# Moving adaLN weight slabs between slots of the RWKV turns, two score-maxima calls into the last turn, and eight square sums behind four more matmul pieces

## What is computed (the reference, cut)

```python
# RWKV heads, after the scan y:
mean = jnp.mean(y, axis=-1, keepdims=True)
yc = y - mean
y = yc * lax.rsqrt(jnp.mean(yc * yc, axis=-1, keepdims=True) + RWKV_GN_EPS)
# dilated attention: scores, then their maximum, then the exponential
m = jnp.max(scores, axis=-1, keepdims=True)
p = jnp.exp(scores - m)
# differential attention of the second block, the norm of each head's output
y = of * lax.rsqrt(jnp.mean(jnp.square(of), axis=-1, keepdims=True) + RMS_EPS) * g * (1.0 - lam_init)
```

## Time and profile before

| | us |
|---|---|
| median of 3 runs | 3110.01 |
| lowest, highest | 3106.93, 3116.91 |
| time of the profiled execution | 3103.57 |
| its span, first to last instruction | 3101.8 |
| TensorE busy | 3001.1 (97%) |
| DVE busy | 1669.6 (54%) |
| ACT busy | 1352.2 (44%) |
| mean granted TensorE clock | 0.989 of full |

### The profile page before, as it was taken

How to read it: one execution, slowest core, us unless ns; L and a number is a source line. 1 busy time by engine, 2 the same in 40 slices (tenths; PEclk the granted TensorE clock), 3 DMA queues, 4 the chain that set the end, 5 groups by cost and what they waited for, 6 DMA issues and landing times.

```text
span 3101.8 us, 48573 instructions
## 1 busy us (share of the span) xinstructions
PE 3001.1 (97%) x19912; PEld 2541.9 (82%) x19912; DVE 1669.6 (54%) x2561; ACT 1352.2 (44%) x2084; POOL 43.8 (1%) x84
## 2 busy tenths in 40 slices
PE   8999998999899999999999999999999999999997
PEld 7877876898588778788888887788888998889896
DVE  6655655544666556564454224554562574256754
ACT  5333333434455445454443224444442461255543
POOL 1000000000000000000000000000000000000000
PEclk9999999999999999999999999999999999999998
DMA  7655655355665776745553222222233442234443
GB/s 273 218 205 208 216 185 214 105 172 224 236 217 188 273 272 233 283 165 180 184 188 113 88 89 82 82 82 92 82 128 107 165 171 87 95 121 148 137 163 109
DMA packets 73800, 510.18 MB, mean 164 GB/s; under 512 B 8325, under 2 KB 8465, under 8 KB 19601
## 3 DMA queue, kind: packets, MB, share of 16 engines
q1 hardware_dynamic: 63504, 435.74, 40.8%
q0 software_dynamic: 10112, 71.73, 6.0%
HBM read 503.23 MB, written 6.55 MB: 164 GB/s over the span
## 4 chain that ended last, share of the span: by engine, by line
PE 91%; DVE 4%; ACT 2%; DMA 2%; issue 1%; SPq 0%; ACTq 0%; DVEq 0%
PE bank L767 21%; PE bank L711 16%; PE bank L710 7%; PE bank L1467 5%; PE bank L1469 5%; PE bank L1468 5%; PE bank L910 3%; PE bank L942 3%; PE bank L911 2%; PE bank L912 2%; PE bank L1050 2%; DMA ring_f<-in_w_mod 2%; PE bank L808 2%; PE bank L809 1%; PE bank L810 1%; PE bank L1118 1%
## 5 line engine op out<-in xcount | busy, mean ns | idle before, releaser
L2285 DVE TENSOR_TENSOR ring_f32r<-ring_f,high_f32r 128x1024 fp32r<-128x1024 f32 (+1 forms) x738 | 830.2, 1163 | 761.9 <-ACT high_f32r L1642 745.4
L1642 ACT CAST high_f32r<-ring_f 128x1024 fp32r<-128x1024 f32 (+1 forms) x644 | 609.3, 994 | 859.0 <-PE bank L767 462.6
L711 PE MATMUL bank<-hyz_f32r,high_f32r 128*128 128x512 f32 x2112 | 752.6, 401 | 3.8 <-DVE hyz_f32r L2285 3.8
L710 PE MATMUL bank<-hyz_f32r,ring_f32r 128*128 128x256 f32 x2008 | 564.8, 281 | 1.8 <-DVE ring_f32r L2285 0.9
L767 PE MATMUL bank<-hyz_f32r,high_f32r 128*128 128x512 f32 (+1 forms) x2016 | 534.9, 343 | 5.2 <-DVE hyz_f32r L2285 3.0
L711 PEld LDWEIGHTS bank<-hyz_f32r,high_f32r 128*128 128x128 f32 x2112 | 394.4, 188 | 122.4 <-issue 34.9
L767 PE MATMUL bank<-hyz_f32r,ring_f32r 128*128 128x512 f32 (+1 forms) x1184 | 411.1, 347 | 0.0
L767 PEld LDWEIGHTS bank<-hyz_f32r,high_f32r 128*128 128x128 f32 x2016 | 348.6, 190 | 49.2 <-issue 6.2
L710 PEld LDWEIGHTS bank<-hyz_f32r,ring_f32r 128*128 128x128 f32 x2008 | 380.4, 189 | 7.6 <-DVE hyz_f32r L2285 1.6
L1467 PE MATMUL bank<-hyz_f32r,high_f32r 128*128 128x512 f32 (+1 forms) x1024 | 359.0, 351 | 2.7 <-DVE ring_f32r L2285 2.7
L1469 PE MATMUL bank<-hyz_f32r,ring_f32r 128*128 128x512 f32 (+1 forms) x1024 | 344.8, 337 | 0.0
(11 more groups left out here) (415 smaller groups left out, 4022.7 us busy)
## 6 DMA issues: line engine op xcount, KB each, us to landing
ring_f<-in_w_in SPq DMA_DIRECT2D x159, 1024.0 KB, 4.9
ring_f<-in_w_up SPq DMA_DIRECT2D x88, 1024.0 KB, 4.9
ring_f<-in_w_out SPq DMA_DIRECT2D x56, 1024.0 KB, 4.9
ring_f<-in_w_mod SPq DMA_DIRECT2D x48, 1024.0 KB, 5.1
ring_f<-in_w_down SPq DMA_DIRECT2D x64, 704.0 KB, 4.1
h_f<-in_w_mod POOLq DMA_DIRECT2D x38, 1024.0 KB, 6.8
ring_f<-in_w_kv SPq DMA_DIRECT2D x8, 1024.0 KB, 5.5
z_f<-in_w_mod POOLq DMA_DIRECT2D x8, 1024.0 KB, 8.2
```

Of the source, the lines that this page charges most:

```text
L710: mm(small, lo, x_hi, start=False, stop=False)
L711: last = mm(bank, hi, pair(x_hi, x_lo), start=start, stop=stop)
L1642: act.copy(w_hi[p % 2][:, half], slot[s % SLOTS][:, half]).then_inc(w_high, 1)
L2285: return v.tensor_tensor(out, in0, in1, op)
```

## The change

The 1st place of each turn is taken out and a new last place is put behind the next turn's first products (`ups_matmuls`), in turn 5 behind `a_scores(0)` and `a_v_turned(0)`; the numbering moves down by one, so that the same slabs are read in the same order. `MOD_STEPS` follows. Before `rw_ops` TensorE takes 7.9 instead of 7.0 us of steps (6.9 instead of 6.0 in the last turn, where `evacuated(2)` has 2.4 instead of 3.2). The two first calls of `a_maxima` move into DVE's last turn, between the group norm's variance and the wait for its root. In layer 1 the sum of squares comes 8 instead of 4 pieces behind the values; the pieces behind it are fewer by 4. Layer 0 stays as it was.

```diff
--- before.py
+++ after.py
@@ -49,7 +49,7 @@
 IN1_EARLY = 6
 IN1_FIRST, IN1_COUNT = (6, 13, 20, 27, 34, 40), (7, 7, 7, 7, 6, 6)
 IN1_LAST = 46
-MOD_STEPS = (31, 50, 57, 65, 73, 82, 91, 103)
+MOD_STEPS = (31, 57, 66, 75, 82, 91, 104, 109)
 TURN_MODS = 8
 NORM_MODS = (8, 4)
 UP_MODS = [3, 6, 9, 12] + [32 + 3 * k // 2 for k in range(16)] + [62 + 4 * k // 3 for k in range(16)]
@@ -1086,10 +1086,9 @@
                 if final:
                     beside1(4.0)
                     sgu_sum("g_made", sgu_t, 1)
-                    beside1(6.0)
+                    beside1(6.9)
                 else:
-                    beside1(7.0)
-                turn_mod(TURN_MODS * i + 1)
+                    beside1(7.9)
                 pe.wait_ge(S("rw_ops"), i + 1)
 
                 def rows(n):
@@ -1108,7 +1107,7 @@
                                       kn[rows(hd), t * P + 64 * j:t * P + 64 * j + 64], start=True, stop=True)
                 last.then_inc(S("rw_prod"), 1)
                 beside1(2.6)
-                turn_mod(TURN_MODS * i + 2)
+                turn_mod(TURN_MODS * i + 1)
                 pe.wait_ge(S("rw_bonus"), i + 1)
                 pe.wait_ge(S("inv_dve"), i * 10 + 1)
 
@@ -1122,12 +1121,12 @@
 
                 def evacuated(dve, act=None):
                     if final and dve in (2, 3):
-                        beside1(3.2 if dve == 2 else 0.0)
+                        beside1(2.4 if dve == 2 else 0.0)
                         sgu_turned(dve - 2)
                     elif final and dve in (5, 7):
                         sgu_mixed(dve // 2 - 2)
                     elif dve in (4, 8):
-                        turn_mod(TURN_MODS * i + 2 + dve // 4)
+                        turn_mod(TURN_MODS * i + 1 + dve // 4)
                     else:
                         beside1(1.6 if dve == 10 else 1.8 if final and dve == 6 else 1.15)
                     pe.wait_ge(S("inv_dve"), i * 10 + dve)
@@ -1180,7 +1179,7 @@
                             last = mm(bk[(5, 2)[j]][rows(hd), t * CH:(t + 1) * CH], tok_vz[rows(j), 1, t, rows(hd)],
                                       m_tt[rows(j), 2 * hd + t, :], start=True, stop=True)
                 last.then_inc(S("rw_nv"), 1)
-                turn_mod(TURN_MODS * i + 5)
+                turn_mod(TURN_MODS * i + 4)
                 pe.wait_ge(S("rw_v_made"), 2 * i + 1)
                 for t in range(2):
                     for hd in range(2):
@@ -1198,7 +1197,7 @@
                     mm(bk[6][:, c * CH:(c + 1) * CH], state, zr[:, t, 1, o:o + 64], start=True, stop=True
                        ).then_inc(S("ch_u"), 1)
                     if c == 1:
-                        turn_mod(TURN_MODS * i + 6)
+                        turn_mod(TURN_MODS * i + 5)
                     else:
                         beside1(0.95)
                     pe.wait_ge(S("ch_U"), i * 4 + (c + 1))
@@ -1216,7 +1215,7 @@
                             mm(out, tok_vz[rows(j), 0, t, rows(hd)], prods[rows(j), hd, 1, t, 1, :], start=False, stop=True)
                 mm(bk[5][:, 0:T], head_ones, bonus, start=True, stop=True).then_inc(S("rw_yi"), 1)
                 beside1(0.6)
-                turn_mod(TURN_MODS * i + 7)
+                turn_mod(TURN_MODS * i + 6)
                 pe.wait_ge(S("gn"), i * 2 + 1)
                 mm(bk[2][:, 0:T], head_ones, yy, start=True, stop=True).then_inc(S("gn_sum"), 1)
                 beside1(1.3)
@@ -1229,6 +1228,7 @@
                     a_v_turned(0)
                 else:
                     ups_matmuls(i + 1)
+                turn_mod(TURN_MODS * i + 7)
                 for _ in pieces:
                     pass
             pieces = last_in1()
@@ -1531,7 +1531,7 @@
 
                 pieces = projection2(layer)
                 per = 16 * PER[layer]
-                before_v = (8, 7)[layer]
+                before_v, after_o = (8, 7)[layer], (4, 8)[layer]
 
                 def beside_it(n):
                     for _ in range(n):
@@ -1563,10 +1563,10 @@
                         c = (4 - keys + kt) * P
                         last = mm(bk[2][:, 0:T], Z5[:, 16 + h, c:c + P], own.at[:, kt, :], start=(kt == 0), stop=(kt == keys - 1))
                     last.then_inc(S("d_o"), 1)
-                    beside_it(4)
+                    beside_it(after_o)
                     pe.wait_ge(S("d_osq"), n + 1)
                     mm(bk[3][:, 0:T], ones, own.sq, start=True, stop=True).then_inc(S("d_ss"), 1)
-                    beside_it(per - used - before_v - 8)
+                    beside_it(per - used - before_v - after_o - 4)
                     g = step - POOL_STEP[layer] - 1
                     if 0 <= g < 4:
                         pe.wait_ge(S("p_diff"), 4 * layer + g + 1)
@@ -2415,6 +2415,18 @@
             dve.wait_ge(S("rwkv_loaded"), 32)
             rwv = vec("rw").rearrange("p (g n) -> p g n", n=16)
             dve.sem_inc(S("rw_y"), 1)
+            def a_maxima(i, hd):
+                dve.wait_ge(S("a_s"), i + 1)
+                if i == 3 and hd == 0:
+                    dve.wait_ge(S("G_loaded"), 32)
+                if i >= 2:
+                    dve.wait_ge(S("a_pt"), 2 * i + hd - 3)
+                b, g, nm, out = bk[2 + hd], G[2 * i + hd], at_nm[i % 2], at_s[i % 2][hd]
+                stt(out[:, 0:T], b[:, 0:T], 0.125, g, op1=ALU.add)
+                step(stt(out[:, T:T + P], b[:, T:T + P], 0.125, g[:, P:T], op1=ALU.add))
+                v.reduce_max(nm[:, 2 * hd + 1:2 * hd + 2], out[:, 0:T], AX.X, negate=True)
+                v.reduce_max(nm[:, 2 * hd:2 * hd + 1], out[:, T:T + P], AX.X, negate=True).then_inc(S("a_max"), 1)
+
             def turn(i):
                 sgu = i == C_TILES - 1
                 step(v.tensor_copy(gp, at(rwv, i)))
@@ -2566,6 +2578,10 @@
                 tt(tmp, yy, yy).then_inc(S("gn"), 1)
                 dve.wait_ge(S("gn_sum"), i * 2 + 2)
                 ts(rinv, bk[3][:, 0:T], 1.0 / HEAD, GN_EPS).then_inc(S("gn_var"), 1)
+                if sgu:
+                    dve.wait_ge(S("G_loaded"), 16)
+                    a_maxima(0, 0)
+                    a_maxima(0, 1)
                 if i < 4:
                     in1_lowered()
                 dve.wait_ge(S("gn_std"), i + 1)
@@ -2581,18 +2597,6 @@
                 turn(i)
             dve.sem_inc(rhs_made, 1)
 
-            def a_maxima(i, hd):
-                dve.wait_ge(S("a_s"), i + 1)
-                if i == 3 and hd == 0:
-                    dve.wait_ge(S("G_loaded"), 32)
-                if i >= 2:
-                    dve.wait_ge(S("a_pt"), 2 * i + hd - 3)
-                b, g, nm, out = bk[2 + hd], G[2 * i + hd], at_nm[i % 2], at_s[i % 2][hd]
-                stt(out[:, 0:T], b[:, 0:T], 0.125, g, op1=ALU.add)
-                step(stt(out[:, T:T + P], b[:, T:T + P], 0.125, g[:, P:T], op1=ALU.add))
-                v.reduce_max(nm[:, 2 * hd + 1:2 * hd + 2], out[:, 0:T], AX.X, negate=True)
-                v.reduce_max(nm[:, 2 * hd:2 * hd + 1], out[:, T:T + P], AX.X, negate=True).then_inc(S("a_max"), 1)
-
             def a_normed(i, hd):
                 dve.wait_ge(S("a_exp"), 2 * i + hd + 1)
                 den, p = at_den[i % 2][:, 2 * hd:2 * hd + 2], at_s[i % 2][hd]
@@ -2614,9 +2618,6 @@
                 dve.sem_inc(S("sum_read"), 1)
                 step(v.reciprocal(stat[:, 0:T], stat[:, 0:T]))
 
-            dve.wait_ge(S("G_loaded"), 16)
-            a_maxima(0, 0)
-            a_maxima(0, 1)
             for i in range(A_TILES - 1):
                 a_maxima(i + 1, 0)
                 a_normed(i, 0)
```

## The result

The changed kernel takes 3083.34 us (median of 4 runs, 3079.92 to 3083.91), the kernel before 3108.47 in the same session: ratio 0.9919, 95% interval 0.9900 to 0.9938, so 25.1 us less. The forecast was 3091 with 3083 to 3101 and "faster": right, but only 0.3 us inside its low end. The profiled execution took 3083.16 us (span 3081.4, against 3101.8), 20.4 less.

What follows compares the result with a forecast made beforehand. TensorE, busy 3001.1 of 3101.8 us, bounds the kernel; only its waits and low clock can be won. Terms -15.4 + 1.5 + 0 + 0.5 + 3.0 - 3.0 - 5.4 = -18.8 from 3110.0 give 3091.2, range 3083 to 3101.

Steps and rivals of the forecast that it cites:

- The late slab: Turns 0 to 4, slab of the old 2nd place: 11.1 us of waits and 4.35 of low clock go, -15.4 us.
- no wait of L942 of over 0.8 us: Sign that the forecast is right: TensorE's slab waits at L942 in turns 0 to 4 stay at most 0.8 us.
- The new last place: Ends of turns 0 to 3: the slab for the moved product lands slightly late, 0.4 x 4 = +1.5 us.
- Filler in turn 4: Chunk 2 of turn 4's scan: 0.9 us of steps are missing while TensorE waits for DVE, +0.5 us.
- The tile load: Turn ends: tile load goes out about 0.5 us later, lands after 7.7, hidden up to 8.3: 0 us.
- the rival's mechanism: Loads in line: tile load behind slabs lands too late for `rw_ops` in turns 1 to 4, total 3117.4; chance 0.03.
- Turn 5: Last turn: step 56 needs a half that DVE subtracts late; products 1.55 us late, then 3.9 idle, low clock: +3.0 us.
- The wait of 2 us before the products: Sign that the forecast is right: in turn 5 TensorE waits 2 us for a subtraction just before L1103.
- The maxima: Attention's start: early score maxima, no 3.03 us gap before `a_scores(1)` and no clock fall behind it: -3.0 us.
- The bound that I gave from DVE's start alone: Small end of the maxima term: only DVE's earlier start on the next maxima counts, -0.6 us.
- The square sums: Layer 1's heads: four waits of 1.35 us in steps 3 to 6 vanish behind four more pieces, -5.4 us.
- turn 5 coming out free: Case used for the low end: step 56's half is there in time, so turn 5's 3.0 us are not lost.

Runs made afterwards that it cites:

- maxima_alone: Only the two first `a_maxima` calls moved, on the kernel before; slab places and square sums as before: 3106.39 us, ratio 0.9996.
- before_again: The kernel before, unchanged, profiled a second time: 3105.53 us.
- tile_later: Changed kernel, but in turns 0 to 3 SP asks for the tile load only after the next turn's first tile (5.8 us later): 3096.53 us.
- places_alone: Only the slabs' places and filler amounts changed, on the kernel before; maxima and square sums as before: 3094.37 us, ratio 0.9962.
- late_maxima: Changed kernel without the early maxima: the two `a_maxima` calls come after `rw_y`, as before: 3085.95 us.
- sums_alone: Only layer 1's square sums moved, behind 8 instead of 4 pieces, on the kernel before: 3102.30 us, ratio 0.9980.

## Why the prediction came out as it did

By the means over the table, the four stretches changed like this; forecast and measured:

| | forecast | measured |
|---|---|---|
| turns 0-4 | -13.4 | 360.2 - 378.9 = -18.7 |
| turn 5 | +3.0 | 88.1 - 83.6 = +4.5 |
| to `pv` | -3.0 | 15.5 - 17.2 = -1.7 |
| layer 1 | -5.4 | 268.3 - 275.3 = -7.0 |
| sum | -18.8 | -22.9 |

(Turn 5's new mean is over profiles with 6.9 us of steps; `to pv` over those with moved product and early maxima, against three of before's code; layer 1 over 8 pieces against 4.) The medians say -25.1; the 2 us that are left are not assigned. The forecast left out that one product changes its column twice: by it, turns 0 to 4 should have had 1.0 less, and turn 5, where the product at the start is not hidden, 1.0 more.

**The late slab** (-15.4 forecast): right in mechanism, too small in size. The forecast took waits and clock from one execution: 13.6 us of waits in the whole kernel and three drops. The other three profiles with the old places have 15.0, 15.4 and 16.7 us, the longest single wait 4.9 (maxima_alone):

```profile
164.75 1.94 PE L942 MATMUL bank<-ring_f,rest_f 128*32 128x512 f32 x8 [4.86 <-DMA ring_f<-in_w_mod]
```

Of the 5.3 us between forecast and mean, 3.2 are that the first profile was quicker in these turns than the mean of the four, 1.0 is the product that left the stretch, and 0.6 comes from the next term.

In the first profile of the changed kernel no wait of L942 of over 0.8 us is left in turns 0 to 4, as I had set it; in the second there is one of 0.88, at the product in chunk 1 of the scan in turn 1, and five other profiles with the new places have 0.76 to 1.16 at that product. The place behind `rw_prod` waits in none. From the first slab behind `rw_prod` to the next it takes 7.6 us in all of them (7.3 forecast). **The new last place**: +1.5 forecast; the distances from that place's predecessor are 6.00 to 6.20 us instead of 5.83, so 0.9 us in four turns. **Filler in turn 4** (+0.5): not seen. Turn 4 takes 70.8 to 71.0 us in six of the nine profiles, and 71.3 in before_again once its slab wait is taken off. **The tile load** at 0 holds, with less to spare than I had: in turn 3 `rw_ops` came 0.6 us before TensorE wanted it, in turns 1, 2 and 4 2.0 to 2.7. tile_later shows the rival's mechanism; its condition, a landing of 11.6 us and more, came true in none of the 32 loads, of which the slowest took 8.7.

**Turn 5** (+3.0): right in mechanism. From step 40 to the last wait the forecast had 18.0 us where the profile of before has 16.4; it is 18.2 in all seven profiles, and 16.1 with one step fewer and the clock at full. The last wait is 3.76 for 3.9. The wait of 2 us before the products is not a sign to rely on: 1.75 in one profile, 0.27 in six. The low clock behind the last wait costs 1.3 to 1.5 us (2.4 in one profile), 1.45 forecast. What the term lacked is turn 4's product at the turn's start, 1.0 us: step 40 comes at 24.9 instead of 23.9 us where the clock is full, at 26.5 instead of 25.3 where it is low. With some 0.4 us of scatter at the end of the turn this makes the 4.5.

**The maxima** (-3.0) is the step that failed. It priced the gap before `a_scores(1)` by a profile in which the clock had fallen behind it, and took that fall, 2 us of it, as a part of every execution; between the two profiles of the same kernel it is worth 2.9. Against the first profile the stretch did get 3.8 us shorter, against the second 0.8. And the whole gain was put down to the early maxima, though the moved product alone fills most of the gap: 0.18 us of waiting are left in places_alone and 1.39 in late_maxima, which have the same code here. The wait's length only tells how fast TensorE came (sums_alone, with the code of before here, has 1.53 instead of 3.03); with late maxima `a_scores(1)` starts 7.2 us behind `a_scores(0)` in every profile. Beside the product the early maxima bring 0.8 us; alone, 1.3 us of total that can't be told from nothing. The bound that I gave from DVE's start alone, 0.6, was the nearest.

**The square sums** (-5.4): the four waits went, and no new wait at the sum. It measures 6.05 us up to the wait at L767, in every pair of profiles. Of that 5.5 are heads 3 to 6, which had the waits, and 0.3 each stands in heads 1 and 2 (counted from 0), whose rows show no wait in either kernel; the cause there is open. The rest of the mean's 7.0 is chance: behind L767 the clock fell in three of the four profiles with four pieces and in one of the eight with eight.

So the signs of the large terms were right and the total was too small by 4 us in the stretches and 6 in the medians. The hit is in part luck: the low end of 3083 was made from turn 5 coming out free, the maxima at -4.3, no cost at the new places and none in turn 4, of which only the last came true, and from 2 us for scatter. What filled the sum instead is the late slab. The forecast moved its level up by 6.4 us, since the profiled execution (3103.6) was quicker than the medians of before (3107 to 3110), but it left the waits as that execution had them. Where an ordinary execution loses those 6.4 us is not shown: in these four stretches together the first profile of before has 753.2 us and the second 753.8.

## What to carry to other kernels

Before a wait is priced from one profile, ask whether it is of a kind that varies (a DMA landing, a clock drop behind it): its gain is to be made from several executions, or given a range on the high side. Two edits that close the same gap are priced together, not one by one. When a stall comes from one filler step too many, try to take away that step before the whole edit: one step fewer gave 0.9 to 2.1 us of turn 5 back, while its old layout lost behind `a_scores(0)` what it won before. Compare distances between the starts of the same two instructions, not the lengths of waits: the wait before turn 5's products was 1.75 or 0.27 us, and the distance 18.2 in both. And when an edit moves work over a boundary at which profiles are cut into stretches, count it in both.

## What the runs showed of the hardware

The same idle time may or may not be followed by a clock drop. In all 14 profiles TensorE waits 2.09 to 2.10 us for DVE at one L767 behind layer 1's heads, with the same instructions around it. In nine of them the next 30 matmuls take 3.7 us, in five 5.1 to 5.2. The kernel before, and places_alone:

```profile
2993.56 0.51 PE L767 MATMUL bank<-hyz_f32r,high_f32r 128*128 128x256 f32 x2 [2.10 <-DVE ring_f32r L2285]
```
```profile
2994.00:2998.00 4.00, 4.00 (x36) 4.00 (x35) 2.45 (x3) 0.69 (x2) 0.00 (x0) 1.00 0.75 291
```
```profile
2981.45 0.74 PE L767 MATMUL bank<-hyz_f32r,high_f32r 128*128 128x256 f32 x2 [2.10 <-DVE ring_f32r L2285]
```
```profile
2982.00:2986.00 4.00, 4.00 (x24) 4.00 (x24) 2.34 (x3) 0.58 (x2) 0.00 (x0) 0.63 0.77 293
```

Each such drop is worth 1.4 to 1.5 us here. The same holds where the code is the same throughout: before and before_again have this wait, once without and once with the drop. What decides between the two is not shown by these runs. Nor is why the first 57.3 us of both profiles of before took 58.3 to 60.7 in eleven of the other twelve (57.4 in sums_12): that part is the same code in all.

A clock drop costs nothing where another engine sets the pace. In turn 5 of the changed kernel TensorE ran at a granted clock of 1.00 behind the first wait in one profile and at 0.67 in the other, and reached the step behind the last wait 18.2 us later in both: the low clock only shortened its next wait, from 1.75 to 0.27 us.
